# Two down units in one load: 14 KB in a row per partition, one signal for both

## The chip, the cores and the metric

The kernel runs on one core of one Trainium2 chip. The metric is the device time of one execution in microseconds (us). A core has TensorE (PE in the profile; PEld is its weight load), VectorE (DVE), ScalarE (ACT), GpSimd (POOL), SyncE (SP, which here only issues transfers) and 16 DMA engines that carry data between the main memory and the on-chip memory of 128 partitions.

## What is computed

Two decoder layers over 256 tokens of width 1024. Each layer has a mixer (convolution, state-space and attention groups), then a channel mixer, then an embedding gate. The channel mixer of the second layer is the part that matters here: eight experts, of which each token takes two.

```python
def swiglu(h, wg, wu, wd):
    return (jax.nn.silu(h @ wg) * (h @ wu)) @ wd

def moe_top2(h, router, wg, wu, wd):
    ...
    logits = (hf @ router).astype(jnp.float32)
    top_val, top_idx = lax.top_k(logits, TOP_K)
    gates = jax.nn.softmax(top_val, axis=-1)
    ...
    def expert_block(args):
        xblk, e = args
        return swiglu(xblk, wg[e], wu[e], wd[e])

    yb = lax.map(expert_block, (xb, block_exp))
    ...

def reference(...):
    for i in range(DEPTH):
        ...                       # mixers
        if i % 2 == 0:
            h = h + swiglu(hn, dense_w_gate[j], dense_w_up[j], dense_w_down[j])
        else:
            h = h + moe_top2(hn, moe_router[j], moe_w_gate[j], moe_w_up[j], moe_w_down[j])
        ...                       # embedding gate
    return rms_norm(h, final_norm_g)
```

An expert has 3 matrices of 1024 x 3584 float32, 44 MB; all eight are 352 MB, each read once.

## The kernel before

**Units.** An expert's weights come in 48 units of 128 partitions x 1792 float32, 7,168 bytes per partition and 896 KB in all (`CHUNK` is 1792, `M_UNITS` is 48). Units 0 to 31 are gate and up, in the order gate, up, gate, up with 8 units each (`M_IN` is 32, `DOWN0` is 32). Units 32 to 47 are the down matrix (`M_DOWNS` is 16): partition p holds 7 rows of it in a row for each of 4 groups, which is 28,672 bytes without a gap in the main memory, cut into `PARTS` = 4 units. `expert_unit` gives the source of a unit, `moe_load` (line 1386) issues its transfer on SP.

**Ring.** The units land in a ring of 8 slots (`M_SLOTS`); unit number m of the stage goes to slot m % 8, and each slot has a semaphore of its own (`mloaded`), which a transfer raises by 16 when it has landed. `moe_landed` says which semaphore and which value stands for unit m.

**Two experts side by side.** Experts are sorted by how many tokens they have, and two run at a time. The one with many tokens is *heavy*: its inputs are split into two parts (high and low) for exact products. ACT copies a heavy unit from the ring to `w_hi` (`moe_split`, line 1483), DVE then writes the remainder into `ring_lo`, which lies over the same bytes as the ring (line 1991), and PE runs three products per tile (lines 637, 638, 639). So a heavy slot is free when PE has read it. The one with few tokens is *light*: PE reads it from the ring as it is (`light_in`, line 1154; `light_down`, line 1168), and no other engine touches it.

**Order.** `BODY` sets the order of loads and of PE's work alike: four heavy units, four light units, and so on, 96 units to a *turn*. The light expert runs 16 units (`LATER`) behind the heavy one. So in each turn the last four heavy groups are down units (with light gate and up units beside them), and in the first four groups of the next turn the light ones are down units. There are four turns; the first has 80 units, and after the last come the 16 light down units that are left (`last_downs` on PE), 384 units in all. The third turn is the body of a loop with a register bound, and the last uses register values too. Between the third and the last heavy down group of a turn PE also gathers the rows of the next experts (`gather`, line 1066, 32 matmuls of 192 columns).

**Who waits for whom.** SP issues strictly in order. Before the load of the unit at place n it waits until the unit at place n - 8, the slot's former content, has been read (`reader_at`, or `tail_back` for the last 16). ACT waits for the landing of each heavy unit (`mloaded`) before its copy; it copies at most 3 heavy units ahead of PE (`MOE_LEAD`). PE waits for DVE (`lo_ready`) at a heavy unit and for the landing itself at a light unit.

## Time and profile before

| what | value |
|---|---|
| median of 3 runs | 1439.19 us |
| lowest, highest | 1438.46, 1440.05 us |
| time of the profiled execution | 1440.5 us |
| its span | 1438.7 us |
| PE busy | 1387.9 us, 96% of the span |
| DVE busy, ACT busy | 854.1 us (59%), 695.3 us (48%) |
| mean granted clock of TensorE | 0.991 |
| expert stage, first load to last landing | 537.3 to about 1395 us |
| loads of expert units | 3 x 128, 896 KB each, median 8.9 to 9.9 us from issue to landing |

The page gives for each engine the time in which it was busy, 40 slices of the span with the busy share in tenths, the chain of work that ended last, and groups of instructions. A timeline lists instructions with their start in us from the span's start, and in brackets how long the engine had been idle and what ended that. A view of one source line gives its instructions in a stretch, and for transfers the time from issue to landing.

### The profile page before, as it was taken

Reading aid. Unit: us, or ns where it says so; the run is one execution under the profiler, and the core shown is the slowest. Engines: PE = TensorE matmul, PEld = TensorE weight load, DVE = VectorE, ACT = ScalarE, POOL = GpSimd, SP = SyncE. Lnnn points to the kernel's source line nnn. Section 1 sums busy time; section 2 is a strip of 40 time slices with the busy share of each in tenths; the row PEclk is TensorE's granted clock in tenths of the full one; section 3 lists DMA queues with packets and bytes.
Section 4 is the critical chain, followed back from the end, with each engine's and each line's share of the span. In section 5 each row is a group of like instructions: output and inputs, shape, how many; then the busy total and the mean of one; then the engine's idle time right before and its main releaser. Section 6 shows DMA issues by size and latency. Waiting matters only on the chain.

```text
span 1438.7 us, 18295 instructions
## 1 busy us (share of the span) xinstructions
PE 1387.9 (96%) x6999; PEld 1007.7 (70%) x6999; DVE 854.1 (59%) x986; ACT 695.3 (48%) x783; POOL 6.9 (0%) x14
## 2 busy tenths in 40 slices
PE   6999999999989998999999999999999999999996
PEld 6878888888887787766666666666666666666535
DVE  6997645463479978646454656454656455565425
ACT  6556534542555657544444444444444454544315
POOL 0000000000000000000000000000000000000000
PEclk9999999999999999999999999999999999999998
DMA  9425565555544009999999999999999999999992
GB/s 326 159 69 172 177 199 180 177 200 181 176 136 146 8 8 418 363 421 419 419 405 418 419 419 420 414 404 419 418 420 418 416 412 419 418 419 419 419 410 80
DMA packets 99669, 443.89 MB, mean 309 GB/s; under 512 B 7728, under 2 KB 22096, under 8 KB 99328
## 3 DMA queue, kind: packets, MB, share of 16 engines
q1 hardware_dynamic: 98688, 439.30, 78.1%
q0 software_dynamic: 896, 3.44, 0.7%
q8 instruction: 56, 0.92, 0.3%
q14 instruction: 29, 0.24, 0.0%
HBM read 440.61 MB, written 2.10 MB: 308 GB/s over the span
## 4 chain that ended last, share of the span: by engine, by line
PE 83%; DMA 7%; DVE 6%; ACT 2%; issue 1%; DVEq 0%; ACTq 0%; SPq 0%
PE psum L637 19%; PE psum L638 18%; PE psum L639 18%; PE psum L1154 11%; PE psum L1168 7%; DMA ring<-in_moe_w_up 4%; DMA ring<-in_moe_w_down 3%; PE psum L682 2%; PE psum L1066 1%; PE psum L700 1%; PE psum L660 1%; ACT w_hi L1483 1%; DVE arena_a L2078 1%; PE psum L1183 1%; DVE ring_lo L1991 1%
## 5 line engine op out<-in xcount | busy, mean ns | idle before, releaser
L1991 DVE TENSOR_TENSOR ring_lo<-ring,w_hi 128x1792 fp32r<-128x1792 f32 x191 | 384.3, 2023 | 281.1 <-ACT w_hi L1483 279.0
L1483 ACT ACTIVATE w_hi<-ring 128x1792 fp32r<-128x1792 f32 x191 | 323.3, 1700 | 289.2 <-DMA ring<-in_moe_w_down 121.1
L639 PE MATMUL psum<-w_hi,hidden_b 128*128 128x512 f32 x624 | 230.1, 369 | 0.0
L1985 DVE TENSOR_TENSOR ring_lo<-ring,w_hi 128x2048 fp32r<-128x2048 f32 (+1 forms) x68 | 152.6, 2266 | 102.5 <-ACT w_hi L1477 102.4
L1154 PE MATMUL psum<-ring,xT 128*64 128x512 f32 (+1 forms) x1024 | 201.7, 543 | 0.0
L637 PE MATMUL psum<-w_hi,hidden_b 128*128 128x512 f32 (+1 forms) x512 | 191.3, 374 | 5.2 <-ACT arena_b L1787 3.4
L638 PE MATMUL psum<-ring_lo,hidden_b 128*128 128x512 f32 (+1 forms) x512 | 187.7, 367 | 0.0
L637 PE MATMUL psum<-w_hi,xT_parts 128*128 128x512 f32 (+1 forms) x384 | 150.4, 392 | 4.0 <-DVE xT_parts L2002 3.4
L637 PE MATMUL psum<-w_hi,hidden_a 128*128 128x512 f32 (+1 forms) x384 | 146.7, 382 | 3.6 <-DVE ring_lo L1991 3.6
L1154 PEld LDWEIGHTS psum<-ring,xT 128*64 128x64 f32 x1024 | 69.8, 137 | 114.1 <-issue 112.0
L639 PE MATMUL psum<-w_hi,xT_parts 128*128 128x512 f32 (+1 forms) x384 | 149.2, 389 | 0.0
L638 PE MATMUL psum<-ring_lo,xT_parts 128*128 128x512 f32 (+1 forms) x384 | 149.1, 388 | 0.0
L638 PE MATMUL psum<-ring_lo,hidden_a 128*128 128x512 f32 (+1 forms) x384 | 143.1, 373 | 0.0
L1477 ACT ACTIVATE w_hi<-ring 128x2048 fp32r<-128x2048 f32 (+1 forms) x68 | 126.3, 1898 | 29.2 <-PE psum L639 27.8
L639 PEld LDWEIGHTS psum<-w_hi,hidden_b 128*128 128x128 f32 x624 | 117.6, 188 | 20.8
L637 PEld LDWEIGHTS psum<-w_hi,hidden_b 128*128 128x128 f32 x512 | 96.8, 189 | 34.0 <-issue 9.5
L1168 PE MATMUL psum<-ring,xT 128*64 128x512 f32 (+1 forms) x512 | 112.8, 545 | 0.6 <-DMA ring<-in_moe_w_down 0.6
L638 PEld LDWEIGHTS psum<-ring_lo,hidden_b 128*128 128x128 f32 x512 | 96.9, 189 | 16.0
L639 PE MATMUL psum<-w_hi,hidden_a 128*128 128x512 f32 (+1 forms) x272 | 99.3, 365 | 0.0
L637 PEld LDWEIGHTS psum<-w_hi,hidden_a 128*128 128x128 f32 x384 | 72.3, 188 | 21.3 <-DVE ring_lo L1991 9.3
L637 PEld LDWEIGHTS psum<-w_hi,xT_parts 128*128 128x128 f32 x384 | 72.7, 189 | 18.4 <-DVE ring_lo L1996 3.6
L639 PEld LDWEIGHTS psum<-w_hi,xT_parts 128*128 128x128 f32 x384 | 72.5, 189 | 14.2
(333 smaller groups left out, 1448.3 us busy)
## 6 DMA issues: line engine op xcount, KB each, us to landing
ring<-in_moe_w_gate SPq DMA_DIRECT2D x128, 896.0 KB, 8.9
ring<-in_moe_w_up SPq DMA_DIRECT2D x128, 896.0 KB, 9.9
ring<-in_moe_w_down SPq DMA_DIRECT2D x128, 896.0 KB, 9.8
ring<-in_w_in SPq DMA_DIRECT2D x16, 1024.0 KB, 5.7
ring<-in_dense_w_gate SPq DMA_DIRECT2D x14, 1024.0 KB, 5.1
ring<-in_dense_w_up SPq DMA_DIRECT2D x14, 1024.0 KB, 5.1
ring<-in_dense_w_down SPq DMA_DIRECT2D x14, 1024.0 KB, 4.9
ring<-in_w_out SPq DMA_DIRECT2D x8, 1024.0 KB, 5.0
```

Of the source, the lines that this page charges most:

```text
L637: mm(o, a[0], b[0], start=first, stop=False)
L638: mm(o, a[0], b[1], start=False, stop=False)
L639: return mm(o, a[1], b[0], start=False, stop=final)
L660: last = mm(o[:, c:c + P], h[:, t, kt * P:kt * P + P], diag[:, t, :], start=True, stop=True)
L682: last = mm(o[:, m * SEQ:m * SEQ + SEQ], w[:, kt, m * P:m * P + P], xT[kt], start=kt == 0, stop=kt == KT - 1)
L700: last = mm(o[:, 0:n], xT[kt][:, t * P:t * P + P], w[:, q, :], start=kt == 0, stop=kt == KT - 1)
L1154: last = mm(psum[half * LIGHT:half * LIGHT + LIGHT, 4 + b, 0:n], xl[:, kt, :], w[:, a:a + n], start=kt == 0, stop=kt == KT - 1)
L1168: last = mm(psum[half * LIGHT:half * LIGHT + LIGHT, 2 if tail else 6, c0:c0 + n], elT(kt), w[:, a:a + n], start=kt == 0, stop=kt == FKT - 1)
L1477: A(high(g, sizes[g]), raw(g, sizes[g]), ACT.Copy).then_inc(hi_ready, 1)
L1483: A(heavy_high(c), moe_raw(m), ACT.Copy).then_inc(hi_ready, 1)
L1985: V.tensor_tensor(low(g, sizes[g]), raw(g, sizes[g]), f32(high(g, sizes[g])), ALU.subtract).then_inc(lo_ready, 1)
L1991: V.tensor_tensor(moe_low(m), moe_raw(m), f32(heavy_high(c)), ALU.subtract).then_inc(lo_ready, 1)
```

## The change

Two neighbouring down units, of even and odd number, are loaded by one transfer into two neighbouring slots: 128 partitions x 3584 float32, 14,336 bytes in a row per partition, 1792 KB. `second(c)` is true for the odd unit of such a pair. It issues nothing, and its readers look at the semaphore of the even slot, which is raised once for both. Gate and up units are loaded as before. Because a slot's semaphore now counts a different number of loads per turn in even and in odd slots, `moe_landed` counts them instead of deriving them from m.

SP waits before such a load for the former reader of the second slot, `n + 1 - M_SLOTS`, where before it waited for each slot's own. The 16 units at the end go in 8 pairs.

```diff
             if c >= DOWN0:
                 group, part = divmod(c - DOWN0, PARTS)
                 rows = d.rearrange("(g p r) n -> p g (r n)", p=P, r=RUN)
-                return rows[:, group:group + 1, part * CHUNK:(part + 1) * CHUNK]
+                return rows[:, group:group + 1, part * CHUNK:(part + 2) * CHUNK]
...
-        def moe_landed(m, i):
-
-            return mloaded[m % M_SLOTS], i * (16 * PAIR_UNITS // M_SLOTS) + 16 * (m // M_SLOTS + 1)
+        def second(c):
+
+            return c >= DOWN0 and c % 2 == 1
+
+        def loads_into(slot, at):
+            return sum(1 for m, c in at if m % M_SLOTS == slot and not second(c))
...
+        def moe_landed(m, i, c):
+
+            m -= second(c)
+            slot = m % M_SLOTS
+            if isinstance(i, int) and i == 0:
+                return mloaded[slot], 16 * loads_into(slot, [(n, u) for n, u in IN_START if n <= m])
+            n = PER_START[slot] - PER_BODY[slot] + loads_into(slot, [(n, u) for n, u in IN_BODY if n <= m])
+            return mloaded[slot], i * (16 * PER_BODY[slot]) + 16 * n
...
-            def moe_load(m, src):
-                sp.dma_start(moe_raw(m).rearrange("p (k n) -> p k n", k=1), src).then_inc(mloaded[m % M_SLOTS], 16)
+            def moe_load(m, src, units=1):
+                a = m % M_SLOTS * CHUNK
+                sp.dma_start(ring[:, a:a + units * CHUNK].rearrange("p (k n) -> p k n", k=1), src).then_inc(
+                    mloaded[m % M_SLOTS], 16)
...
-                    else:
-                        sp.wait_ge(*reader_at(i, n - M_SLOTS))
+                    c = light_at(0, s)[1] if k else s
+                    if second(c):
+                        continue
+                    if n >= M_SLOTS or not (isinstance(i, int) and i == 0):
+                        sp.wait_ge(*reader_at(i, n + (c >= DOWN0) - M_SLOTS))
                     which = (light if s >= LATER else light_before) if k else heavy
-                    moe_load(base + n, expert_unit(*which, light_at(0, s)[1] if k else s))
+                    moe_load(base + n, expert_unit(*which, c), 2 if c >= DOWN0 else 1)
...
-            for j in range(M_DOWNS):
-                sp.wait_ge(*tail_back(n_iter, j, M_SLOTS))
-                moe_load(j - M_DOWNS, expert_unit(*last, DOWN0 + j))
+            for j in range(0, M_DOWNS, 2):
+                sp.wait_ge(*tail_back(n_iter, j + 1, M_SLOTS))
+                moe_load(j - M_DOWNS, expert_unit(*last, DOWN0 + j), 2)
...
             def moe_split(i, c, m):
 
-                act.wait_ge(*moe_landed(m, i))
+                act.wait_ge(*moe_landed(m, i, c))
```

SP's queue, at the first group of heavy down units of the first turn. ISA is a wait that stands by itself; `unit_used` and `u_full` are raised by PE when it has read a heavy unit, `light_used` and `lu_full` when it has read a light one. Before:

```order
L1386 DMA ring<-in_moe_w_up 128x1792 [waits light_used] x4
L1386 DMA ring<-in_moe_w_down 128x1792 [waits unit_used] x2
L1386 ISA [waits unit_used]
L1386 DMA ring<-in_moe_w_down 128x1792
L1386 ISA [waits u_full]
L1386 DMA ring<-in_moe_w_down 128x1792
L1386 ISA [waits light_used]
L1386 DMA ring<-in_moe_w_gate 128x1792
```

Now:

```order
L1414 DMA ring<-in_moe_w_up 128x1792 [waits light_used] x4
L1414 DMA ring<-in_moe_w_down 128x3584 [waits unit_used]
L1414 ISA [waits u_full]
L1414 DMA ring<-in_moe_w_down 128x3584
L1414 ISA [waits light_used]
L1414 DMA ring<-in_moe_w_gate 128x1792
```

Four loads with four waits have become two loads with two waits, those for the readers of the second and the fourth slot; the order of everything else is the same.

ACT's queue in the first turn, copies of heavy units at the change from up to down units; `mloaded0` to `mloaded3` are the semaphores of the four slots that heavy units use. Before:

```order
L1483 ACTIVATE w_hi<-ring 128x1792 [waits unit_used,mloaded0]
L1483 ACTIVATE w_hi<-ring 128x1792 [waits g_full,mloaded1]
L1483 ACTIVATE w_hi<-ring 128x1792 [waits unit_used,mloaded2]
L1483 ACTIVATE w_hi<-ring 128x1792 [waits unit_used,mloaded3]
L1483 ACTIVATE w_hi<-ring 128x1792 [waits unit_used,mloaded0]
L1483 ACTIVATE w_hi<-ring 128x1792 [waits unit_used,mloaded1]
L1483 ACTIVATE w_hi<-ring 128x1792 [waits unit_used,mloaded2]
L1483 ACTIVATE w_hi<-ring 128x1792 [waits unit_used,mloaded3]
```

Now:

```order
L1515 ACTIVATE w_hi<-ring 128x1792 [waits unit_used,mloaded0]
L1515 ACTIVATE w_hi<-ring 128x1792 [waits g_full,mloaded1]
L1515 ACTIVATE w_hi<-ring 128x1792 [waits unit_used,mloaded2]
L1515 ACTIVATE w_hi<-ring 128x1792 [waits unit_used,mloaded3]
L1515 ACTIVATE w_hi<-ring 128x1792 [waits unit_used,mloaded0] x2
L1515 ACTIVATE w_hi<-ring 128x1792 [waits unit_used,mloaded2] x2
```

The copies stand where they stood; the first copy of a pair now waits for the signal of both units, and the second for the same one. On PE the order of the matmuls is unchanged, 16 rows that compute a semaphore value in a register are added in the third and fourth turns, and the second light down unit of a pair waits for the even slot's semaphore.

## Rows read from the trace of the kernel before

**Rows 1.** the page: span, TensorE's busy time, DMA engines' busy tenths in 40 slices.

```profile
span 1438.7 us, 18295 instructions
...
PE 1387.9 (96%) x6999; PEld 1007.7 (70%) x6999; DVE 854.1 (59%) x986; ACT 695.3 (48%) x783; POOL 6.9 (0%) x14
...
DMA  9425565555544009999999999999999999999992
```

**Rows 2.** stretches: busy us per engine, then TensorE's clock, DMA share, GB/s.

```profile
660.00:855.00 195.00, 193.61 (x970) 127.20 (x968) 104.15 (x72) 90.80 (x77) 0.00 (x0) 1.00 1.01 416
...
880.00:1091.00 211.00, 209.72 (x1053) 137.64 (x1052) 116.65 (x84) 97.39 (x80) 0.00 (x0) 1.00 1.01 416
1091.00:1303.00 212.00, 211.16 (x1059) 138.75 (x1058) 116.16 (x81) 97.25 (x80) 0.00 (x0) 1.00 1.01 417
```

**Rows 3.** who PE waited for, 660 to 1340 us: total us, times, longest.

```profile
PE psum L1080 <- DVE h L2502: 3.8, 3, 1.8
PE psum L637 <- DVE ring_lo L1991: 1.5, 2, 1.4
```

**Rows 4.** ACT's timeline, heavy down copies: start, us, instruction, [idle before].

```profile
868.04 1.70 ACT L1483 ACTIVATE w_hi<-ring 128x1792 fp32r<-128x1792 f32 x1 [9.23 <-DMA ring<-in_moe_w_down]
870.24 1.70 ACT L1483 ACTIVATE w_hi<-ring 128x1792 fp32r<-128x1792 f32 x1 [0.49 <-DMA ring<-in_moe_w_down]
```

**Rows 5.** timelines: remainder and first matmul of a heavy down group's first unit.

```profile
657.51 2.02 DVE L1991 TENSOR_TENSOR ring_lo<-ring,w_hi 128x1792 fp32r<-128x1792 f32 x1 [2.38 <-ACT w_hi L1483]
...
659.59 0.50 PE L637 MATMUL psum<-w_hi,hidden_a 128*128 128x512 f32 x1 [1.37 <-DVE ring_lo L1991]
...
904.72 2.03 DVE L1991 TENSOR_TENSOR ring_lo<-ring,w_hi 128x1792 fp32r<-128x1792 f32 x1 [5.24 <-ACT w_hi L1483]
...
907.11 0.19 PEld L637 LDWEIGHTS psum<-w_hi,hidden_a 128*128 128x128 f32 x1 [0.60 <-DVE ring_lo L1991]
...
1119.05 0.50 PE L637 MATMUL psum<-w_hi,hidden_a 128*128 128x512 f32 x1 [0.15 <-DVE ring_lo L1991]
...
1348.39 0.50 PE L637 MATMUL psum<-w_hi,hidden_a 128*128 128x512 f32 x1 [2.11 <-DVE ring_lo L1991]
```

**Rows 6.** single transfers of line 1386: when issued, and us to landing.

```profile
L1386 SPq DMA_DIRECT2D ring<-in_moe_w_down x1: 333/333/333, 729.7 to 729.7; - x1
...
DMA to landing us min/median/max: 7.9/7.9/7.9
...
L1386 SPq DMA_DIRECT2D ring<-in_moe_w_down x1: 336/336/336, 942.3 to 942.3; - x1
...
DMA to landing us min/median/max: 7.4/7.4/7.4
...
L1386 SPq DMA_DIRECT2D ring<-in_moe_w_down x1: 332/332/332, 1153.9 to 1153.9; - x1
...
DMA to landing us min/median/max: 8.0/8.0/8.0
...
L1386 SPq DMA_DIRECT2D ring<-in_moe_w_gate x1: 333/333/333, 594.7 to 594.7; - x1
...
DMA to landing us min/median/max: 4.8/4.8/4.8
```

**Rows 7.** line 1386 on SP: its register instructions, ns min/median/max.

```profile
L1386 SPq FUSED_REGOPS  x74: 37/37/42, 602.7 to 898.4; - x74
```

**Rows 8.** DMA: slices of 168:184 (2 KB rows); packets of 980:1040 us.

```profile
GB/s 189 307 317 394 410 410 394 113 0 0 0 0 0 0 36 67 195 328 404 410 410 404 343 26 0 0 0 0 61 92 184 353 410 410 404 410 271 26 0 0
...
DMA packets 3937, 25.12 MB, mean 419 GB/s; under 512 B 437, under 2 KB 437, under 8 KB 3931
```

**Rows 9.** timeline of the last two light down units and ACT's next copy.

```profile
1392.75 1.93 PE L1168 MATMUL psum<-ring,xT 128*64 128x512 f32 x8 [0.25 <-DMA ring<-in_moe_w_down]
...
1395.02 1.94 PE L1168 MATMUL psum<-ring,xT 128*64 128x256 f32 x8 [0.34 <-DMA ring<-in_moe_w_down]
...
1397.79 1.91 ACT L1890 ACTIVATE w_hi<-ring 128x2048 fp32r<-128x2048 f32 x1 [0.20 <-DMA ring<-in_ple_w_gate]
```

More of the change, by code:

```diff
@@ L600, in landed, with unit_at, last_landed @@
             return 16 * (g // SLOTS + 1)
-        def moe_landed(m, i):
-            return mloaded[m % M_SLOTS], i * (16 * PAIR_UNITS // M_SLOTS) + 16 * (m // M_SLOTS + 1)
+        def unit_at(n):
+            k, s = BODY[n]
+            return light_at(0, s)[1] if k else s
+        def second(c):
+            return c >= DOWN0 and c % 2 == 1
+        def loads_into(slot, at):
+            return sum(1 for m, c in at if m % M_SLOTS == slot and not second(c))
+        IN_BODY = [(n - LATER, unit_at(n)) for n in range(len(BODY))]
+        IN_START = [(n, s if not k else light_at(0, s)[1]) for n, (k, s) in enumerate(START)]
+        PER_BODY = [loads_into(slot, IN_BODY) for slot in range(M_SLOTS)]
+        PER_START = [loads_into(slot, IN_START) for slot in range(M_SLOTS)]
+        def moe_landed(m, i, c):
[5 more added lines that the diff above has]
+            return mloaded[slot], i * (16 * PER_BODY[slot]) + 16 * n
+        def last_landed(j, i):
+            slot = (j - j % 2) % M_SLOTS
+            return mloaded[slot], i * (16 * PER_BODY[slot]) + 16 * (PER_START[slot] - PER_BODY[slot] + j // M_SLOTS + 1)
         used_before_moe = []
@@ L1142, in light_in @@
                 m = ring_light(c)
-                pe.wait_ge(*moe_landed(m, i))
+                pe.wait_ge(*moe_landed(m, i, c))
                 if c == 0:
@@ L1160, in light_down @@
                 m = ring_light(DOWN0 + j) if not tail else j - M_DOWNS
-                pe.wait_ge(*moe_landed(m, i + 1))
+                pe.wait_ge(*(last_landed(j, i + 1) if tail else moe_landed(m, i + 1, DOWN0 + j)))
                 group, part = divmod(j, PARTS)
@@ L1826, in _ @@
                     first_heavy(0)
-                    act.wait_ge(*moe_landed(0, 0))
+                    act.wait_ge(*moe_landed(0, 0, 0))
                     act.wait_ge(*high_reader(0, 0))
```

## Prediction

> **What bounds the kernel now.** The page says first that TensorE is busy 96% of the span, and the DMA digits say that the DMA engines are full from the fifteenth of 40 slices on [rows 1]. So in the expert stage two things are full at once, and the busy shares can't tell which one sets the time. The view by stretches shows both side by side: from 660 us on PE is busy 99% of each stretch, at the full clock, while the DMA share is 1.01 and 416 to 417 GB/s arrive [rows 2]. The view of waits settles it. Between 660 and 1340 us PE waited 1.5 us for DVE's remainder of a heavy unit and 3.8 us for DVE's add into h [rows 3], in 680 us. PE sets the time, and the DMA engines keep up with almost nothing to spare. Faster transfers alone can therefore give back little; what counts is whether a unit arrives late.
>
> How late may it be? Heavy units land 2.2 us apart (870.24 - 868.04), and ACT had been waiting for each of them [rows 4]. From landing to a readable remainder it takes 1.7 us on ACT and 2.0 us on DVE [rows 4, 5], some 3.8 us with the signals. PE reads the first unit of a heavy group as follows [rows 5]: at 659.59 us it starts 0.06 us after DVE's end (657.51 + 2.02) and had been idle 1.37 us; at 907.11 us it starts 0.36 us after DVE's end (904.72 + 2.03), so 0.3 us are to spare; at 1119.05 us it had waited 0.15 us; at 1348.39 us it had waited 2.11 us. These four places are groups of heavy down units, one in each turn, and they have next to no slack. Light units rest in the ring far longer. A round of eight slots takes 8 x 2.2 = 17.6 us, a load takes up to 9.9 us of it from issue to landing (the median in the table above), so some 7.7 us lie between landing and the end of the reading, of which PE reads for 1.9 us [rows 9].
>
> **The change, part by part.**
>
> *Fewer and longer transfers.* 128 down units become 64 transfers. SP's issue of one takes 0.33 us [rows 6], but SP mostly waits for PE, so 64 x 0.33 us less on SP is worth nothing. What a 14 KB row saves on the DMA engines no row shows; it is bounded by shorter ones. Loads with 2 KB rows reach 410 GB/s in their fullest slices, 7 KB rows run at 419 GB/s in the mean [rows 8]. A row 3.5 times as long gave 2.2%, so a doubling from 7 KB gives between nothing and that: between 0 and 0.10 us of the 4.4 us of a pair. I take the middle, 0.05 us a pair, because the 2 KB bursts are short and their slices coarse. That is 3.2 us of DMA time for 64 pairs, none of it on PE's path by itself.
>
> *One signal for both.* The first unit of a pair can be used when the second has landed, 2.2 us later than now [rows 4]. For light pairs the 5.8 us of rest in the ring cover this. For the second pair of a heavy group PE's own pace covers it: a turn of 96 units takes 211 us [rows 2], so a heavy and a light unit take 4.4 us together and a heavy one some 2.5 us, and PE comes to the third unit after two of these. For the first pair nothing covers it in the groups without slack: ACT, queued in order, begins 2.2 us later, DVE after it, and PE, which has just ended its light units, stands still. In the first turn PE falls back by 2.2 us at 659.59. It doesn't fall back again in the next groups, since it now comes later by itself; but as PE has no idle time to lose, it doesn't catch up either. I call this PE's lag.
>
> *The later issue.* SP waits for the reader of the second slot, so the pair is issued when now its second load is. What is queued behind it in SP comes later anyway. The DMA engines run dry if this comes too late. A load into an empty queue took 4.8 us from issue to landing [rows 6], so to keep the cadence the second load's issue must precede the landing of the first unit by 4.8 us. The closest places are the first light down pairs of a turn, right after the gathers. Now the second load's issue is 7.9, 7.4 and 8.0 us ahead of its own landing [rows 6] and so 5.7, 5.2 and 5.8 us ahead of the first unit's. Its slot comes free with PE's lag on top. So the transfers fall back too: by PE's lag less the 0.9, 0.4 or 1.0 us to spare. With that, the next turn's heavy down units land late, and the 2.2 us are due again.
>
> *The sum*, as lags in us against the kernel before. First turn, PE: 2.2. Second turn, DMA: 2.2 - 0.9 = 1.3, less eight light pairs (0.4) = 0.9; PE: 0.9 + 2.2 - 0.3 of slack - five heavy pairs (0.25) = 2.55. Third turn, DMA: 2.55 - 0.4 - 0.4 = 1.75; PE, without slack: 1.75 + 2.2 - 0.25 = 3.7. Last turn, DMA: 3.7 - 1.0 - 0.4 = 2.3; PE at 1348.39: 2.3 + 2.2 - seven pairs (0.35) = 4.15. The 2.11 us that PE waited there before don't help, since they were a wait for these same units.
>
> *The end.* The last two units now land together. Before, PE read each as it came, 1.93 us apiece, with 0.25 and 0.34 us of waiting [rows 9]; afterwards it has both to read from the last landing on, 1.9 us more. By the DMA's way the end comes at 2.3 - 0.8 (16 more pairs) + 1.9 = 3.4 us, by PE's at 4.15 - 0.6 = 3.55 us. The later one counts, so about +3.6 us, and everything behind it (ACT's next copy at 1397.79 [rows 9], the last gate, the output) shifts along.
>
> *Waits against a register.* 16 register rows are new on PE. On SP such a row takes 37 ns [rows 7]; 0.6 us if none were hidden. PE's sequencer runs ahead of its matmuls, so I take 0.1.
>
> The profiled execution took 1440.5 us at a span of 1438.7; the median is 1.3 us lower. The sum is a difference, and it is carried over to the median: 1439.2 + 3.7 = 1442.9 us.
>
> **A rule that speaks for the change.** The landings follow each other without a pause at 896 KB per load [rows 4, 2]. The Trainium skill, "DMA: Bandwidth & Descriptors", section "Rules for kernel authors", wants 128 partitions and at least 1 MiB per DMA for the highest bandwidth; 896 KB is just below it, 1792 KB above. By that rule the stage would gain. The trace doesn't bear it out, since with loads behind one another the fixed part of one lies under the next.
>
> **The rivals.**
>
> *A longer row is worth much more, and the kernel gets faster.* Mechanism: a pair saves far more than 0.05 us, so that the landings run ahead of PE and no heavy unit is late after the first turn. 41 pairs lie on the path of the sum (8 light ones in each of three turns, 5, 5 and 7 heavy ones), so 0.21 us a pair makes it 3.7 - 41 x 0.16 = -2.9 us, and from there this case decides. It ends where PE has nothing more to wait for: its waits at 659.59 and 1348.39 and a few tenths elsewhere are some 4 us [rows 5]. That gives about 1436 us. For it: the DMA engines are full. Against it: 410 and 419 GB/s [rows 8] leave no such reserve, and PE has little to gain [rows 3]. This is also what the rule above would do here. 7%.
>
> *The lag doesn't build up.* If the DMA engines never run dry, PE loses 2.2 us once, meets later landings that are a little early by then, and gets it back at 1348.39, where it waited 2.11 us [rows 5]. The time is 1438.7 us, no change. It needs a load to be able to land 3.5 us after its issue (5.7 - 2.2); the nearest row says 4.8 [rows 6]. 15%.
>
> *The longer row saves nothing, or is moved as two.* Then the change doesn't do what it says: the sum loses its 41 x 0.05 = 2.1 us, giving +5.7, and if a pair's landing takes 0.3 us more than a single one in each of three turns and the queue also runs dry once among the last heavy pairs, it is +7, 1446 us. 21%.
>
> **How the numbers follow.** My forecast has 57%, with a range of its own from 1440.8 (0.10 us a pair) to 1445 us (nothing saved). A measurement of this kernel tells about 0.2%, 2.9 us, from no change; the forecast's centre lies beyond that by a little, so I give two thirds of it to slower. Slower: 0.36 + 0.21 = 0.57. Within 0.2%: 0.21 + 0.15 = 0.36. Faster: 0.07. The range from 1438.6 to 1446.5 takes in the second rival and nearly all of the third, and leaves out the first.
>
> **What the next profile would show.** Right, if in heavy down groups two copies of ACT stand back to back after an idle time some 2 us longer than now; if PE waits for DVE's remainder about 3 us in all at 659 us and 1 to 1.5 us in each of the later turns; if the DMA share has gaps right after the gathers, where now it is 1.01 throughout; and if the last 16 matmuls of line 1168's successor run without a pause after the last landing. Wrong, if PE's waits don't grow (then the units were not late), if landings after the gathers keep their cadence (then only 2.2 us can be lost), or if the pairs land less than 4.2 us apart (then a longer row is worth more than I took).

## The result and the profile after

| | before | after |
|---|---|---|
| median | 1438.83 us (4 runs) | 1462.51 us (4 runs) |
| lowest, highest | 1438.36, 1440.05 | 1459.79, 1466.11 |
| span of the profiled execution | 1438.7 us | 1464.3 us |
| PE busy | 1387.9 us | 1395.7 us |
| mean granted clock of TensorE | 0.991 | 0.987 |

The changed kernel is slower: the ratio is 1.0162, with a 95% interval from 1.0146 to 1.0179. That is 23.7 us; the prediction said 3.7. Its range ended at 1446.5 us. The profiled execution was the longest of the four (1466.1 us).

The page of the changed kernel, first against [rows 1]:

```profile
span 1464.3 us, 18110 instructions
...
PE 1395.7 (95%) x6999; PEld 1012.4 (69%) x6999; DVE 852.6 (58%) x986; ACT 693.1 (47%) x783; POOL 6.9 (0%) x14
...
DMA  9415556565542039999999999999999999999991
GB/s 330 156 58 173 198 174 200 174 199 190 175 138 93 8 123 410 372 422 362 397 406 417 418 418 390 381 406 416 419 414 395 390 411 418 403 394 393 406 413 66
```

The DMA digits still say 9 and more, and would let one believe that nothing happened. The line below them shows it: of the 21 slices from the nineteenth to the last but one, twelve stand at 362 to 406 GB/s. In the kernel before two of them do, at 404 and 405, and the others stand at 410 to 420. A slice is 37 us long, and its digit doesn't resolve a loss of 5%.

The same stretches as in [rows 2], with two more around the longest wait:

```profile
661.90:667.30 5.40, 5.35 (x16) 4.48 (x17) 5.07 (x4) 3.29 (x2) 0.00 (x0) 0.50 1.01 418
667.30:673.00 5.70, 5.70 (x32) 4.85 (x32) 2.51 (x2) 0.60 (x2) 0.00 (x0) 0.97 0.61 219
660.00:855.00 195.00, 191.51 (x944) 127.85 (x946) 102.95 (x70) 88.08 (x75) 0.00 (x0) 0.98 0.99 402
880.00:1091.00 211.00, 206.22 (x1028) 136.25 (x1030) 111.78 (x78) 93.40 (x78) 0.00 (x0) 1.00 1.00 405
1091.00:1303.00 212.00, 204.63 (x1017) 133.10 (x1014) 113.83 (x83) 96.94 (x80) 0.00 (x0) 0.99 1.00 404
```

PE was busy for 2.1, 3.5 and 6.5 us less in the long stretches, and 402 to 405 GB/s arrive where 416 to 417 did. From 661.9 to 667.3 us the clock is at the lower of its two levels (0.50), and right behind that the DMA engines are idle for 2.2 of 5.7 us.

Who PE waited for between 660 and 1360 us (total us, times, longest), against [rows 3]:

```profile
PE psum L664 <- DVE ring_lo L2023: 16.0, 12, 3.5
PE psum L1107 <- DVE h L2534: 3.9, 3, 1.8
PE psum L1100 <- DVE h L2534: 1.7, 2, 1.6
PE psum L1210 <- DVE hidden_a L2033: 1.5, 2, 0.8
```

Line 664 is the former 637, line 1107 the former 1080. Before there were two waits for the remainder of a heavy unit, 1.5 us in all; now there are twelve with 16.0 us. The stretch ends 20 us later than that of [rows 3], since the same work is reached that much later; taken to 1360 us, the kernel before has three such waits with 3.6 us. The wait for h at line 1107 has stayed what it was; those at lines 1100 and 1210, 3.2 us in all, are nearly all new (0.3 us at the former 1183 before). PE's timeline gives the places:

```profile
661.95 0.80 PE L664 MATMUL psum<-w_hi,hidden_a 128*128 128x512 f32 x1 [3.46 <-DVE ring_lo L2023]
...
700.48 0.50 PE L664 MATMUL psum<-w_hi,hidden_a 128*128 128x512 f32 x1 [1.17 <-DVE ring_lo L2023]
...
879.84 0.50 PE L664 MATMUL psum<-w_hi,hidden_a 128*128 128x512 f32 x1 [1.82 <-DVE ring_lo L2023]
...
916.86 0.50 PE L664 MATMUL psum<-w_hi,hidden_a 128*128 128x512 f32 x1 [1.30 <-DVE ring_lo L2023]
...
924.02 0.50 PE L664 MATMUL psum<-w_hi,hidden_a 128*128 128x512 f32 x1 [2.04 <-DVE ring_lo L2023]
```

The first is the place and nearly the size that the prediction gave it (1.37 before, plus 2.2). The others shown are new, and there are more like them; those at 916.86 and 924.02 us are the first and the second pair of one and the same group. ACT's timeline shows the pairs as forecast, two copies in one row of 3.28 us behind one landing:

```profile
658.14 3.28 ACT L1515 ACTIVATE w_hi<-ring 128x1792 fp32r<-128x1792 f32 x2 [11.34 <-DMA ring<-in_moe_w_down]
```

Compare the 9.23 us of idling in [rows 4]. How fast the loss builds up is seen at a matmul that stands once in each turn from the second on, in `scatter_light`. It is line 1080 of the kernel before:

```profile
855.66 0.50 PE L1080 MATMUL psum<-hidden_b 64*128 64x512 f32 x2 [1.79 <-DVE h L2502]
...
1067.36 0.50 PE L1080 MATMUL psum<-hidden_b 64*128 64x512 f32 x2 [1.28 <-DVE h L2502]
...
1278.74 0.51 PE L1080 MATMUL psum<-hidden_b 64*128 64x512 f32 x2 [0.69 <-DVE h L2502]
```

and line 1107 of the changed one:

```profile
861.25 0.50 PE L1107 MATMUL psum<-hidden_b 64*128 64x512 f32 x2 [1.07 <-DVE h L2534]
...
1079.51 0.51 PE L1107 MATMUL psum<-hidden_b 64*128 64x512 f32 x2 [1.04 <-DVE h L2534]
...
1298.06 0.51 PE L1107 MATMUL psum<-hidden_b 64*128 64x512 f32 x2 [1.80 <-DVE h L2534]
```

The changed kernel is later by 5.6, 12.2 and 19.3 us: 6 to 7 us are lost per turn, again and again. A mechanism that costs something once and then carries it along would not look like this.

### The profile page after: what moved, and what is told of

It is laid out like the page before. It is cut to its first block, busy times and chain, and to the rows that moved or that the text cites. A ratio compares the mean times of both kernels' runs of the same rounds, so it can differ in the third digit from the quotient of the medians.

```text
span 1464.3 us, 18110 instructions
## 1 busy us (share of the span) xinstructions
PE 1395.7 (95%) x6999; PEld 1012.4 (69%) x6999; DVE 852.6 (58%) x986; ACT 693.1 (47%) x783; POOL 6.9 (0%) x14
## 4 chain that ended last, share of the span: by engine, by line
PE 75%; DMA 13%; DVE 7%; ACT 3%; issue 2%; DVEq 0%; ACTq 0%; SPq 0%
PE psum L664 18%; PE psum L665 17%; PE psum L666 17%; PE psum L1181 8%; DMA ring<-in_moe_w_down 7%; PE psum L1195 6%; DMA ring<-in_moe_w_up 5%; ACT w_hi L1515 2%; PE psum L709 2%; DVE ring_lo L2023 2%; PE psum L1093 1%; PE psum L727 1%; PE psum L687 1%; DVE arena_a L2110 1%; PE psum L1210 1%
## 5 line engine op out<-in xcount | busy, mean ns | idle before, releaser
L1509 ACT ACTIVATE w_hi<-ring 128x2048 fp32r<-128x2048 f32 (+1 forms) x68 | 126.4, 1898 | 28.8 <-PE psum L666 27.8
L664 PEld LDWEIGHTS psum<-w_hi,hidden_b 128*128 128x128 f32 x512 | 97.2, 190 | 35.0 <-issue 10.3
```

Source lines behind the costliest of these rows:

```text
L664: mm(o, a[0], b[0], start=first, stop=False)
L1509: A(high(g, sizes[g]), raw(g, sizes[g]), ACT.Copy).then_inc(hi_ready, 1)
```

## The experiments

All times are differences to the kernel before on the same chip in the same session, with 95% intervals. In the diffs, a line with - is the kernel that the sentence ahead names.

**Which pairs?** Two kernels made of the changed one, in which a unit belongs to a pair only if its expert is of one kind. `k` is 1 for light.

```diff
+        def in_pair(k, c):
+            return c >= DOWN0 and k in (1,)        # (0,) in the other kernel
...
-            return c >= DOWN0 and c % 2 == 1
+            return in_pair(k, c) and c % 2 == 1
```

Light pairs alone:

> Only the down units of the light expert are loaded in pairs (32 of the 64 pairs, the 16 units at the end among them); heavy down units are loaded one by one as before. The changed kernel took 23.7 us more than the kernel before. Theory 1, the loss arises where ACT and DVE stand between the landing and TensorE (heavy pairs): this kernel costs at most what the end costs, +1 to +4 us over before, 1440 to 1443 us, and the page shows steady transfer digits over the whole stage. Theory 2, every pair costs alike because the transfers themselves or their later issue starve the DMA engines: half of the loss, +10 to +13 us, 1449 to 1452 us.

Measured: +4.7 us (2.7 to 6.9), at the upper end of theory 1 and far from theory 2. Heavy pairs alone:

> The counterpart: only the heavy expert's down units are loaded in pairs (32 pairs), the light ones and the end one by one. Theory 1 (the heavy path): nearly all of the loss, +18 to +23 us over before, 1457 to 1462 us, with several TensorE waits in each stretch of heavy down units. Theory 2 (every pair alike): +10 to +13 us. If the two losses do not add up to 23.7 us, the parts interact through the ring.

Measured: +22.4 us (19.0 to 26.0). Together they make 27.1, against 23.7 with both, so they add up within the intervals. The loss is made at the heavy pairs, those that have ACT and DVE between a landing and PE. Theory 2 falls.

**Which side of the pairing?** The pairing does three things: it issues later, it signals later, and it makes one transfer with long rows. The next kernels do one or two of these to the kernel before. Later issue:

```diff
-                        sp.wait_ge(*reader_at(i, n - M_SLOTS))
+                        c = light_at(0, s)[1] if k else s
+                        sp.wait_ge(*reader_at(i, n + (c >= DOWN0 and c % 2 == 0) - M_SLOTS))
...
-                sp.wait_ge(*tail_back(n_iter, j, M_SLOTS))
+                sp.wait_ge(*tail_back(n_iter, j + (j % 2 == 0), M_SLOTS))
```

> The kernel before with its single loads of 7,168 bytes per partition and their own signals; only SyncE waits, before the first load of every pair of down units, for the reader of the second slot, as the changed kernel does. Theory A, the later issue is what drains the DMA engines' work ahead: most of the loss, +14 to +24 us over before. Theory B, the late signal of the first unit does it: at most +3 us here, since a load that is issued about 2.2 us later still has two or three loads ahead of it. Theory C, the long row or the size of one transfer does it: 0 to +1 us.

Measured: +5.3 us by the ratio (2.7 to 8.1), with eight runs spread from 1439.7 to 1449.4 us; the profiled one has a span of 1438.4 us, no longer than that of the kernel before. So the later issue alone is nothing in some executions and up to 11 us in others. Theory A, as it was put then, fails.

Later signal:

```diff
                 act.wait_ge(*moe_landed(m, i))
+                if c >= DOWN0 and c % 2 == 0:
+                    act.wait_ge(*moe_landed(m + 1, i))
...
                 pe.wait_ge(*moe_landed(m, i + 1))
+                if j % 2 == 0:
+                    pe.wait_ge(*moe_landed(m + 1, i + 1))
```

> The kernel before with its single loads issued each at its own time; only the readers of the first unit of a pair (ACT for a heavy one, TensorE for a light one) wait until the second unit has landed too, as one signal for both makes them. Theory A (the issue): at most +5 us over before, single waits of TensorE at the head of heavy down groups and none of the transfers late by more than that. Theory B (the signal): +14 to +24 us. Theory C (row and size): 0 to +3 us. If A and B are each far below the loss and together too, the two need each other: the late signal delays the reader, and the reader delays the issue.

Measured: +12.2 us (9.8 to 14.7), half of the loss. PE waited 11.0 us for remainders between 600 and 1400 us (4.1 before):

```profile
PE psum L637 <- DVE ring_lo L1995: 11.0, 7, 3.6
```

Neither side alone makes the 23.7 us. Both sides, with two transfers still:

> The kernel before with both sides of the pairing at once and nothing else: SyncE waits for the second slot's reader before the first load of a pair (alone it cost +4.0 us in the median, with a profiled span of 1438.4 us, that of before), and the readers of the first unit wait for the second's landing too (alone +12.1 us). Each unit is still a transfer of its own with rows of 7,168 bytes. Theory A, the ring: a slot is held 2.2 us longer on each side, the two add up on the same round of the ring, and once that round is longer than the eight units take, both count in full: 1458 to 1464 us, the changed kernel's time. Theory B, the signals alone: as one signal alone, 1449 to 1453 us, and the missing 12 us are the price of the 1792 KB transfer or of its 14 KB rows. If it is simply additive: 1454 to 1456 us.

Measured: +28.8 us (26.3 to 31.2), more than the changed kernel and far more than the 17.5 of the two parts' sum. The two sides need each other. And one large transfer with short rows; here the second half of a pair comes from the next row group:

```diff
-                group, part = divmod(c - DOWN0, PARTS)
+                part, group = divmod(c - DOWN0, 4)
...
-                return rows[:, group:group + 1, part * CHUNK:(part + 2) * CHUNK]
+                return rows[:, group:group + 2, part * CHUNK:(part + 1) * CHUNK]
...
-                sp.dma_start(ring[:, a:a + units * CHUNK].rearrange("p (k n) -> p k n", k=1), src).then_inc(
+                sp.dma_start(ring[:, a:a + units * CHUNK].rearrange("p (k n) -> p k n", k=units), src).then_inc(
```

> The changed kernel, but a pair is made of the same stretch of two neighbouring row groups of the down matrix, so that each partition's 14,336 bytes come from two places of 7,168 bytes. The size of a transfer, its issue and its signal are those of the changed kernel; the data reach other slots than the matmuls expect, so the output is not the reference's. Theory A, long rows cost nothing and save 9 ns a row: 1462 to 1468 us, as slow as the changed kernel or up to 5 us slower. Theory C, rows of 14 KB are themselves bad for the transfers: 1440 to 1455 us.

Measured: +30.2 us (27.6 to 32.9), the same within the intervals as two loads under both conditions. So the size of a transfer costs nothing that these runs can tell, and the long row gives something back, 6.5 us by the difference of the two kernels' excess (30.2 - 23.7), to which the intervals leave some 3 us either way. The landings agree: where a pair was issued more than 5 us ahead of the landing before it, it landed 4.293 us behind that (median of 27) with long rows and 4.367 us (27) with short ones, twice the 2.184 us of a single load. That is 0.074 us a pair, 4.7 us for 64.

**Is the second pair of a group covered?** The prediction said so. Only ACT's wait, and only at the first or only at the third unit of the heavy down groups (`c % 4 == 0` or `c % 4 == 2`):

> The kernel before, in which only ACT, and only at the first of the four units of each heavy down group, waits for the landing of the unit behind it (16 places in all); light units, and the third unit of a group, are read as before. The prediction counted the late signal at this place alone, since the second pair of a group was held to be covered. Theory 1 (the prediction's accounting): the cost of one signal at all pairs, +12.1 us, is made here, +9 to +13 us, and the same wait at the third unit costs 0 to +1. Theory 2 (every pair has the same few tenths of slack): half or less of it here, +4 to +7 us.

> The kernel before, in which only ACT, and only at the third of the four units of each heavy down group, waits for the landing of the unit behind it (16 places). Theory 1 (the prediction's accounting, this wait is covered by the two units ahead of it): 0 to +1 us, no wait of TensorE that the kernel before does not have. Theory 2 (every pair has the same small slack): +4 to +7 us with waits of 0.5 to 1.5 us at the third units. If first and second together stay below 12.1 us, the light expert's late signals carry the rest.

Measured: +8.8 us (6.3 to 11.2) at the first and +8.2 us (5.8 to 10.5) at the third unit. There is no covered pair. The waits differ in kind. Late at the third unit, PE had waited for remainders only 5.6 us in seven times, but 3.5 us for `hidden_a`, where it was 0.3 us in the kernel before:

```profile
PE psum L637 <- DVE ring_lo L1993: 5.6, 7, 1.4
PE psum L1080 <- DVE h L2504: 4.2, 3, 1.6
PE psum L1183 <- DVE hidden_a L2003: 3.5, 4, 0.9
```

`hidden_a` holds the heavy expert's hidden rows. ACT makes their high part (line 1842 of the changed kernel) in one order with the copies of units, so a copy that starts 2.2 us late pushes back what stands behind it, and DVE's part after that. That last step is read from the order of ACT's work; it wasn't tried by itself.

**One side, twice as long.** The later issue by two slots, nothing else. This tells a sum of two different troubles from one quantity with an edge:

```diff
-                        sp.wait_ge(*reader_at(i, n - M_SLOTS))
+                        c = light_at(0, s)[1] if k else s
+                        sp.wait_ge(*reader_at(i, n + 2 * (c >= DOWN0 and c % 2 == 0) - M_SLOTS))
...
-                sp.wait_ge(*tail_back(n_iter, j, M_SLOTS))
+                sp.wait_ge(*tail_back(n_iter, j + 2 * (j % 2 == 0), M_SLOTS))
```

> The kernel before with single loads, own signals and own readers; SyncE waits, before the first load of every pair of down units, for the reader two slots further (not one). That holds a slot about 4.4 us longer on the side of the issue alone; the late issue by one slot cost 0 to 4 us, the late signal 12.1 us, both together 29.5 us. Theory A, what counts is the whole round of a slot (issue, flight, split, products, issue again) against the time in which eight units arrive, whichever side is made longer: the same 4.4 us cost about as much as both together, +20 to +30 us. Theory D, it is the late signal that counts, since it alone reaches TensorE, and the issue only adds to it: +4 to +10 us, with transfers landing late but few waits of TensorE.

Measured: +32.4 us (29.2 to 35.4). 2.2 us on this side cost 5, 4.4 us cost 32, and 2.2 on each side cost 29. With 4.4 us it hardly matters on which side a slot is held, and the second 2.2 us are much dearer than the first. With 2.2 us it does matter, 5.3 against 12.2. This is what theory A said of the round, a little above its 20 to 30.

**Take 1.4 us out again.** The changed kernel, with ACT copying 256 of 1792 columns of each heavy down unit:

```diff
-                A(heavy_high(c), moe_raw(m), ACT.Copy).then_inc(hi_ready, 1)
+                n = 256 if c >= DOWN0 else CHUNK
+                A(heavy_high(c)[:, 0:n], moe_raw(m)[:, 0:n], ACT.Copy).then_inc(hi_ready, 1)
```

> The changed kernel, in which ACT copies only 256 of the 1792 columns of each heavy down unit (about 0.3 instead of 1.7 us), so that the remainder is ready about 1.4 us sooner after the landing; the other columns keep what stood there, and the output is not the reference's. TensorE, DVE and the transfers do the same work as in the changed kernel. Theory A (a slot's round is too long by a small amount, and everything beyond it is paid at every pair): taking 1.4 of the added 4.4 us out gives back more than half of the loss, 1444 to 1452 us. If the loss were in the transfers themselves: 1460 to 1464 us, no change. With the before kernel's own waits for the split, at most 3.6 us of the gain could come without the pairs.

Measured: +14.4 us (12.2 to 16.4), so 9.3 of the 23.7 us came back. The direction is theory A's, the size is not: it had said more than half, and at most 1452 us where 1453.1 was measured. What is left is that the shorter copy helps the heavy units alone, and up to 3.6 us of the gain may be waits that the kernel before has too.

**Seven slots.** If the round of a slot is what counts, it should be tight without any pair as well:

```diff
-                        sp.wait_ge(*reader_at(i, n - M_SLOTS))
+                        sp.wait_ge(*reader_at(i, n + 1 - M_SLOTS))
...
-                sp.wait_ge(*tail_back(n_iter, j, M_SLOTS))
+                sp.wait_ge(*tail_back(n_iter, j + 1, M_SLOTS))
```

> The kernel before, in which every load of the expert stage (gate and up units too) waits for the reader one slot further, as if the ring had seven slots; single loads, own signals. It makes the round of every slot 2.2 us longer on the issue's side, where the late issue at down pairs did so at 64 of 384 loads for +4.0 us or less. Theory A1, the round is tight everywhere and each load that is issued less than about 5 us before the landing of the one ahead of it lands late by some tenths: +25 us or more. Theory A2, the round is tight only where heavy down units stand (leads of 6 us and more elsewhere): +2 to +10 us.

Measured: +21.4 us (19.0 to 23.9). And with `n + (c < DOWN0) - M_SLOTS`, at gate and up units alone:

> The same one slot later, but at the gate and up units only (256 of the 384 loads); all down units are issued as before. Theory A1: at least half of what seven slots at every load cost. Theory A2: 0 to +3 us. Together with the late issue at down pairs it tells whether the edge lies in the stretches of heavy down units, where the changed kernel took its late issue and its late signal, or in the ring as a whole.

Measured: +19.3 us (15.7 to 22.9). Seven slots at every load cost less than the 25 us that theory A1 named and twice the 10 that A2 allowed, and the gate and up loads alone cost nearly all of it. So A1 holds in its mechanism and is too high in its number: the round is tight everywhere, not in the stretches of heavy down units alone. The GB/s line with seven slots has dips like those of the changed kernel, now all over the stage:

```profile
GB/s 334 154 58 171 200 174 198 176 196 185 178 139 99 9 114 395 346 405 412 394 405 419 400 399 407 391 412 418 401 395 410 390 409 420 406 399 410 419 411 92
```

**The clock.** 14 small matmuls ahead of the wait at 661.95 us:

```diff
+                if j == 0 and isinstance(i, int) and i == 0:
+                    for _ in range(14):
+                        mm(psum[:, 6, 384:512], ident, ident, start=True, stop=True)
                 pe.wait_ge(lo_ready, turn_of(i, c) + 1)
```

> The changed kernel with 14 more matmuls of 128 x 128 (results unused, in a free part of a bank) ahead of the first heavy down unit of the first turn, where TensorE waited 3.5 us for the split and its clock stood at half speed in the 6.8 us that followed. They fill most of that wait. If the waiting is what lets the clock fall, the half-speed stretch at about 660 us is gone and all that follows comes 3 to 3.4 us sooner: 1458 to 1460 us. If the clock falls for another reason, the stretch stays, 1462 to 1464 us. If the extra matmuls outlast the wait, it is up to 1 us slower than that.

Measured: +24.2 us (22.2 to 26.3), no change. The mechanism was there and the gain was not. The stretch at half speed is gone, as the windows of this kernel show (the clock stands third from the end):

```profile
655.00:662.00 7.00, 6.66 (x47) 4.21 (x42) 1.19 (x3) 2.66 (x2) 0.00 (x0) 1.00 0.99 416
662.00:667.00 5.00, 3.85 (x20) 3.30 (x21) 4.66 (x3) 3.91 (x3) 0.00 (x0) 1.00 1.02 420
667.00:673.00 6.00, 6.00 (x34) 5.10 (x33) 4.56 (x5) 1.20 (x2) 0.00 (x0) 1.00 0.99 367
```

Yet what is computed fast here is waited for later, and two shorter stretches at half speed came at 863 and 1355 us. At this place the low clock was a companion of the long wait, not a cost of its own; the other place in the changed kernel (1299 us) was not tried. TensorE was at half speed in the expert stage for 10.2 us in the changed kernel (at 661 and 1299 us), and in the kernel before only in 3.4 us at its beginning (569 us), which both have.

**The end.** Pairs for the last 16 light down units alone:

```diff
-            for j in range(M_DOWNS):
-                sp.wait_ge(*tail_back(n_iter, j, M_SLOTS))
-                moe_load(j - M_DOWNS, expert_unit(*last, DOWN0 + j))
+            for j in range(0, M_DOWNS, 2):
+                sp.wait_ge(*tail_back(n_iter, j + 1, M_SLOTS))
+                moe_load(j - M_DOWNS, expert_unit(*last, DOWN0 + j, 2), 2)
```

> The kernel before, in which only the 16 light down units at the end are loaded in 8 pairs. The prediction put this end at +1.9 us: the last landing carries two units, so that twice the matmuls come behind it. Theory 1: +1.5 to +2.5 us, with the last matmuls of the stage starting that much later after the last landing. Theory 2, the eight saved issues and longer rows (0.08 us a pair) make up for part of it: +0.5 to +1.5 us. No difference: below 0.5 us.

Measured: +1.2 us (-0.4 to 2.7). It doesn't tell the two theories from each other or from nothing. PE's timeline of this kernel shows the last 16 matmuls in one piece:

```profile
1388.08 3.65 PE L1171 MATMUL psum<-ring,xT 128*64 128x512 f32 x16 [0.35 <-DMA ring<-in_moe_w_down]
1392.44 3.65 PE L1171 MATMUL psum<-ring,xT 128*64 128x512 f32 x16 [0.72 <-DMA ring<-in_moe_w_down]
```

None of these kernels beats the kernel before. Light pairs and the end alone come nearest, and the 0.074 us that each pair saves is not seen in their times.

## Why the prediction was wrong

**What the runs put in the place of its account.** A slot goes round: its load is issued, lands, the unit is split and read, the next load is issued. Eight units arrive in 8 x 2.184 = 17.5 us, and a round that needs more holds up the stage. From the trace, for the first and the third unit of the heavy down groups (16 of each), in us, the time from landing to the next issue in its slot, and the time from issue to landing:

```
                     landing to next issue   issue to landing
                     shortest   median       median
first unit
  before               6.5        7.2          10.3
  late issue alone     9.0        9.6           7.9
  late signal alone    8.8        9.5           8.6
  both, two loads     11.2       11.3           7.0
third unit
  before               7.1        8.3           9.3
  late issue alone     9.4       11.0           6.5
  late signal alone    9.0       10.6           7.8
  both, two loads     11.3       12.4           6.5
```

Each side adds some 2.3 us to the left, and the right gives way, since that is where a load had time to spare. The question is how far it can. The prediction took 4.8 us, as the time of a load into an empty queue [rows 6]. (That load had one ahead of it with 1.7 us still to go. The first load of the stage, at 537.3 us with nothing under way, took 4.7 us, so the number stands.) The runs say otherwise. For each load of the stage I took the time by which its issue came ahead of the landing before it, and by how much its own landing then missed the regular step (2.184 us). Over the nine kernels that have single transfers only:

```
issued ahead of the previous landing by    loads   mean delay of the landing, us
over 5 us                                   2906   0.03
4 to 5 us                                    317   0.12
3 to 4 us                                    147   0.43
under 3 us                                    77   1.0
```

By the prediction's 4.8 us, less the step of 2.2, a lead of 2.6 us should do. It takes 4 to 5, that is 6.2 to 7.2 us from issue to landing. This is an edge in the mean and not for each load: over 5 us 4% of the loads were late by more than 0.2 us, at 4 to 5 us 16%, at 3 to 4 us 48%, below that 84%. What the prediction's rule leaves out is large: in the kernel with both sides it would give the short leads a delay of 4.0 us in all, and it was 30.5.

The 6.2 to 7.2 us taken off the 17.5 leave a budget of 10.3 to 11.3 us from landing to the next issue, as an estimate. First units are held for 7.2 us in the kernel before, for about 9.5 with one side and 11.3 with both; third units for 8.3, then 10.6 and 11.0, then 12.4. So one side alone comes to the edge at third units, and with both sides all units come to it or beyond. It also fits seven slots at every load: heavy gate and up units are held for 8.6 to 9.3 us in the median before, by their place in the group, and 2.2 more brings them to 10.8 and beyond.

How much of the loss this carries, by the loads whose issue came less than 5 us ahead. The regular step is 2.184 us, for a pair 4.293 us and with short rows 4.367. The delays are those of the profiled execution, so its own span stands beside them:

```
                      such   their delay   more than   its span,     measured,
kernel                loads  in all, us    before      more than     ratio of
                                                       before        the runs
before                  33       6.5
late issue              55       7.9          1.4        -0.3          5.3
late signal             54      17.6         11.1        11.0         12.2
  first unit only       51      12.1          5.6         5.8          8.8
  third unit only       45       9.7          3.2         4.5          8.2
both, two loads         57      30.5         24.0        28.8         28.8
later by two            81      37.5         31.0        33.2         32.4
seven slots             96      29.4         22.9        22.8         21.4
  gate and up only      69      25.3         18.8        17.1         19.3
short rows              64      32.4         25.9        25.9         30.2
changed kernel          65      34.5         28.0        25.6         23.7
```

For the changed kernel the long rows give back 4.7, and 28.0 - 4.7 = 23.3. The delays of all loads together are the lengthening of the stage by the way they are counted; what the table shows is that nearly all of it falls on the loads with a short lead. This is an account of where the time went, taken from one execution of each; that the shortened lead causes it rests on the kernels that changed nothing but the issue (later by two, seven slots).

**Point by point.**

- *What bounds the kernel.* Right as far as it went: PE sets the time and the DMA engines have nothing to spare. What it missed is the third thing, that the ring is as full as both. The 7.7 us "between landing and the end of the reading" were read as slack of the units; they were the ring's budget.
- *Fewer and longer transfers.* Taken at 0.05 us a pair within 0 to 0.10; measured 0.074. Right in size. It counted only because the transfers now set the pace.
- *One signal for both.* The first wait was right: 3.46 us where 1.37 + 2.2 = 3.6 was due. Two claims failed. "PE doesn't fall back again in the next groups": it waited 1.17 us at 700.48 us and again at 916.86 and 924.02 us. "PE's own pace covers the second pair": late signals at the third units alone cost 8.2 us where the prediction has nothing, and at the first units alone 8.8.
- *The later issue.* This is the step that made the size wrong, together with the second pair that was held to be covered. It sought the places where a load is issued 4.8 us before the first unit's landing, found the ones behind the gathers, and gave 0.9, 0.4 and 1.0 us to spare. Delays begin at 6 to 7 us, not at 4.8, and there were 33 such loads already in the kernel before. Twelve of them are the four loads right behind each gather (from 719.3, 931.5 and 1143.5 us), with leads of 3.4 to 4.9 us: gate units, where the prediction looked at down pairs only. The first heavy down pairs of the first turn show it. The two transfers from SP's line 1414 were issued at 669.7 and 675.5 us, each into a queue that was nearly empty (the load ahead had 1.4 and 0.9 us to go), since PE's wait at 661.95 us had held up their slots:

```profile
L1414 SPq DMA_DIRECT2D ring<-in_moe_w_down x1: 333/333/333, 669.7 to 669.7; - x1
...
DMA to landing us min/median/max: 6.8/6.8/6.8
```

  In the kernel before, the two units of the first of these transfers had been issued at 662.3 and 664.8 us with 11 us to landing:

```profile
L1386 SPq DMA_DIRECT2D ring<-in_moe_w_down x1: 333/333/333, 662.3 to 662.3; - x1
...
DMA to landing us min/median/max: 11.3/11.3/11.3
```

  The DMA engines' idle 2.2 us at 667.3 to 673 (above) lie just there, in the groups of heavy down units, where the prediction expected no gap.
- *The sum* carried one lag from turn to turn and added 1 to 1.5 us each time. The measured steps are 5.6, 6.6 and 7.2 us. A late PE holds up slots, late loads hold up PE, and in a ring without slack each of the eight heavy down pairs of a turn can start this anew. The prediction judged each turn by the one place of [rows 5].
- *The end.* Foreseen +1.9. In the changed kernel the matmuls behind the last landing take 3.65 us where they took 1.94 [rows 9]:

```profile
1417.88 3.65 PE L1195 MATMUL psum<-ring,xT 128*64 128x512 f32 x16 [0.43 <-DMA ring<-in_moe_w_down]
```

  So 1.7 us as such, but by the kernel with pairs at the end alone +1.2 us (-0.4 to 2.7), which agrees both with it and with no cost at all. The 0.6 us that the prediction takes off PE's way there (4.15 - 0.6) has no working in it and no run tests it.
- *The rule on large transfers.* The Trainium skill, "DMA: Bandwidth & Descriptors", section "Rules for kernel authors", wants at least 1 MiB per DMA. With the size doubled and all else equal (short rows against two loads) the times are the same within the intervals, 30.2 and 28.8 us more than before, so no gain is seen here. The same section says to issue a DMA early and to wait late; here that is the rule which the change broke, and the one with a price.
- *The rivals.* The faster one fell. The one in which the lag doesn't build up fell too, since it built up far more than forecast. The one that doubted the saving of the row was wrong in its mechanism. No rival asked what happens if the ring's slack ends.
- *What the next profile would show.* The copies in pairs and the first wait came as told, the later waits not ("1 to 1.5 us in each of the later turns", they are more), and the DMA gaps lie mostly elsewhere than said: the loads issued in the 30 us from each gather's start were late by 7.5 us in all, against 3.5 before, which is some 4 us of the loss.

**What stays open.** Why landings are late by 0.2 us in the mean with a lead of 3 to 5 us, where 2.6 would do by the time of a load into an empty queue. Fetches of instructions travel through the same DMA engines (16 KB at a time, some 1.06 us on one engine, every 25 us or so). Among the 464 loads with such a lead, those during which a fetch began were late by 0.33 us (131 loads), the others by 0.17 (333), so this is a part at most. It wasn't found in the trace what is. Why the later issue alone is nothing in one execution and 11 us in another wasn't settled either. It lies next to the edge, and its profiled execution was one of the two shortest. That `hidden_a` is what makes the late signal at the third unit dear was not tried by itself.

## What to carry to other kernels

Count the round of a buffer before changing it: slots times the time between arrivals must cover the time from issue to landing that keeps the queue full, the splitting, the reading, and every signal. Merging two loads takes one arrival time out of this round twice, on the side of the issue and on that of the signal, and each alone costs far less than both (here 5.3 and 12.2 us against 28.8). Busy shares and DMA digits don't show whether anything is left of it; one kernel in which every load waits for the reader one slot further does, and it is a small change.

## What the runs showed of the hardware

- To land on time, in the mean, in a steady stream of 896 KB loads, a load had to be issued 6 to 7 us ahead of its landing (0.03 us late with a lead over 5 us, 0.12 with 4 to 5, 0.43 with 3 to 4, 1.0 below), although the first one, into an empty queue, took only 4.7 us. This was not expected, and the prediction's error rests on it in large part.
- A row of 14,336 bytes instead of two of 7,168 saved 0.074 us of 4.367 us, 1.7%. The size of the transfer (896 or 1792 KB) made no difference that these runs can tell.
- In the changed kernel a wait of TensorE of 3.46 us that ended at 661.95 us stood beside 6.8 us at the lower clock level (from 660.8 us), and one of 1.80 us that ended at 1298.06 beside 3.4 us (from 1299.1); one of 2.04 us that ended at 924.02 was followed by none. With the first of these waits mostly filled, the 6.8 us were gone and the loss in time was the same, 24.2 against 23.7 us.
